# Routed experts in blocks of 32 slots on four column strips of the matrix array instead of blocks of 64 on two

## The reference, cut to what matters

```python
logits = xf @ w_router + b_router
top_val, top_idx = lax.top_k(logits, TOP_K)            # 4 of 32
top_w = jax.nn.softmax(top_val, axis=-1)
...
def expert_block(args):                                # the tokens of one expert, padded
    xb, e = args
    gate = xb @ w_gate[e] + b_gate[e]
    up = xb @ w_up[e] + b_up[e]
    gate = jnp.minimum(gate, SWIGLU_LIMIT)
    up = jnp.clip(up, -SWIGLU_LIMIT, SWIGLU_LIMIT)
    glu = gate * jax.nn.sigmoid(SWIGLU_ALPHA * gate)
    return ((up + 1.0) * glu) @ w_down[e] + b_down[e]
...
y = jnp.zeros((N, D)).at[tok_sorted].add(rows * w_sorted[:, None])
```

## Time and profile before

| | |
|---|---|
| median of 3 runs | 2026.03 us (2024.24 to 2029.33) |
| the profiled execution, its own time | 2019.1 us |
| its span in the trace | 2017.4 us |
| mean granted clock of TensorE, share of 2.4 GHz | 0.929 |
| experts' stage, first gate matmul to VectorE's last sum | 879.7 to 1985.0 us |
| TensorE busy / weight loads busy / VectorE / ScalarE | 89% / 47% / 32% / 15% |
| read from HBM | 486.86 MB |

### The profile page before, as it was taken

The page is one execution under the profiler, slowest core; times in us unless marked ns, Lnnn a source line. Parts: engine busy times, 40 slices in busy tenths (PEclk is TensorE's granted clock), DMA queues, the critical chain, the costliest instruction groups (busy, mean ns, idle before and its releaser), DMA issues. The chain is left out here.

```text
span 2017.4 us, 22708 instructions
## 1 busy us (share of the span) xinstructions
PE 1803.5 (89%) x8638; PEld 940.3 (47%) x8639; DVE 637.8 (32%) x1142; ACT 301.3 (15%) x521; POOL 126.1 (6%) x198
## 2 busy tenths in 40 slices
PE   6997998999879994589999999999999999999996
PEld 4775766868446762553333333333333333333332
DVE  1454333361410024733133333322332212232222
ACT  2234131110111001121011111111110100111002
POOL 1111202112100005200000000000000000000000
PEclk8998999997689997699998999999999999999997
DMA  9352162210255332049899999998999779898720
GB/s 325 129 167 84 42 233 101 84 53 1 61 184 206 117 147 96 0 192 421 311 379 414 421 422 422 422 422 342 417 417 390 298 292 365 311 410 336 250 83 28
DMA packets 114943, 494.07 MB, mean 245 GB/s; under 512 B 9931, under 2 KB 27532, under 8 KB 65687
## 3 DMA queue, kind: packets, MB, share of 16 engines
q1 hardware_dynamic: 112906, 490.69, 62.8%
q10 hardware_dynamic: 1984, 2.64, 0.4%
HBM read 486.86 MB, written 6.43 MB: 245 GB/s over the span
## 5 line engine op out<-in xcount | busy, mean ns | idle before, releaser
L1710 PE MATMUL ps_moe<-ring,hT_moe 128*64 128x512 f32 x1280 | 308.6, 641 | 0.0
L1710 PE MATMUL ps_moe<-ext,xg 128*64 128x512 f32 x1280 | 281.8, 595 | 3.5 <-DVE xg L1809 3.5
L1710 PE MATMUL ps_moe<-ring,xg 128*64 128x512 f32 x1280 | 281.7, 595 | 0.0
L739 PE MATMUL ps_mix<-hT,ring 128*128 128x320 f32 x896 | 263.2, 450 | 14.7 <-ACT cbuf L656 6.7
L739 PEld LDWEIGHTS ps_mix<-hT,ring 128*128 128x128 f32 x896 | 174.9, 198 | 90.7 <-issue 15.8
L1710 PEld LDWEIGHTS ps_moe<-ring,hT_moe 128*64 128x64 f32 x1280 | 95.4, 147 | 187.6 <-issue 185.0
L1710 PEld LDWEIGHTS ps_moe<-ext,xg 128*64 128x64 f32 x1280 | 91.8, 137 | 180.5 <-issue 177.5
L1710 PEld LDWEIGHTS ps_moe<-ring,xg 128*64 128x64 f32 x1280 | 89.2, 137 | 178.4 <-issue 178.3
L1836 DVE TENSOR_SCALAR gate<-ps_moe 128x1024 f32<-128x1024 f32 x32 | 39.2, 1224 | 233.7 <-PE ps_moe L1717 233.7
L1845 DVE TENSOR_SCALAR hid<-ps_moe 128x512 f32<-128x512 f32 x64 | 44.0, 687 | 209.8 <-PE ps_moe L1717 209.8
L1822 DVE TENSOR_SCALAR chosen<-ones,expert_row 96x64 bf16<-96x64 f32 x32 | 8.0, 250 | 313.8 <-PE ps_moe L1717 313.8
(11 more groups left out here) (354 smaller groups left out, 1711.1 us busy)
## 6 DMA issues: line engine op xcount, KB each, us to landing
ext<-in_w_gate SPq DMA_DIRECT2D x128, 1024.0 KB, 9.9
ring<-in_w_up SPq DMA_DIRECT2D x128, 1024.0 KB, 10.9
ring<-in_w_down SPq DMA_DIRECT2D x128, 1024.0 KB, 8.4
ring<-in_w_in SPq DMA_DIRECT2D x18, 2048.0 KB, 9.1
ring<-in_w_ada SPq DMA_DIRECT2D x12, 2048.0 KB, 9.3
ext<-in_state_gdn_rec SPq DMA_DIRECT2D x8, 512.0 KB, 8.4
out_rec_sample<-ext SPq DMA_DIRECT2D x8, 512.0 KB, 3.2
ring<-in_w_branch_b SPq DMA_DIRECT2D x2, 2048.0 KB, 15.0
```

What stands on the lines that cost most here:

```text
L739: last = nc.tensor.matmul(out, ring[:, place(i), k, P * j:P * j + P], rhs[:, k, :], start=k == 0, stop=k == NC - 1)
L1710: last = nc.tensor.matmul(ps[MID * a:MID * a + MID, bank + blk, :], lhs(blk, c), w[:, k, HALF * a:HALF * a + HALF], start=c == 0, stop=False)
```

## The change

The block of tokens becomes 32 slots wide (STRIP = 32, four blocks in CAP), and each matmul takes a quarter of the output columns (QW = 256) to one of four 32-column strips of the array. A block's product is then 8 chunks by 4 strips. Every PSUM tile of 128 by 512 holds two blocks of 128 by 256. The number of blocks is chosen among 1, 2 and 4: block 1 runs if there are more than 32 tokens, blocks 2 and 3 if there are more than 64, and block 0 always and last. Only block 0 signals that a piece is used. The scatter sums work on four row strips of 32 slots each; they always add blocks 0 and 1, and 2 and 3 for over 64 tokens. The hidden transposes and the put transposes are always made for all four blocks; the put transposes are split in two parts, of which the second stands behind the down product. `sig` shares its memory with `hid`, and `slots` lies in an older buffer.

```diff
-MID = CAP // 2
+NBLK = CAP // STRIP
+Q = NSTRIP
+QW = D // Q
...
-                            for blk in range(blocks):
-                                for a in range(2):
-                                    last = nc.tensor.matmul(ps[MID * a:MID * a + MID, bank + blk, :], lhs(blk, c),
-                                                            w[:, k, HALF * a:HALF * a + HALF], start=c == 0, stop=False)
...
-                        last.then_inc(piece_t, 1)
+                def strips(m, bank, blk, lhs, wait):
+                    for c in range(NC):
+                        if c % 2 == 0:
+                            wait(4 * m + c // 2)
+                        w = raw_piece(ring, ext, 4 * m + c // 2)
+                        for q in range(Q):
+                            last = nc.tensor.matmul(ps[STRIP * q:STRIP * q + STRIP, bank + blk // 2,
+                                                       QW * (blk % 2):QW * (blk % 2) + QW],
+                                                    lhs(blk, c), w[:, c % 2, QW * q:QW * q + QW], start=c == 0, stop=False)
+                        if blk == 0 and c in (1, 3, 5):
+                            last.then_inc(piece_t, 1)
...
+                def product(i, m, bank, n_tok, b, lhs, ready=None):
+                    with pe.If(n_tok > CAP * b + STRIP):
+                        block_of(i, m, bank, 1, lhs, ready)
+                    with pe.If(n_tok > CAP * b + 2 * STRIP):
+                        for blk in (2, 3):
+                            block_of(i, m, bank, blk, lhs, ready)
+                    block_of(i, m, bank, 0, lhs, ready).then_inc(piece_t, 1)
+
+                def sums(i, j, banks, n_tok, b):
+                    def block(blk):
+                        for q in range(Q):
+                            last = nc.tensor.matmul(ps[:, banks[q], 0:T], yrow[STRIP * q:STRIP * q + STRIP, blk, P * j:P * j + P],
+                                                    put[STRIP * q:STRIP * q + STRIP, blk, :], start=blk == 0, stop=blk == 1)
+                        return last
+                    block(0)
+                    with pe.If(n_tok > CAP * b + 2 * STRIP):
+                        block(2)
+                        block(3)
+                    block(1).then_inc(comb_t, 1)
...
                 def body(i, e, b, first_of_pass):
-                    by_width(mine, lambda blocks: product(i, 0, 0, blocks, ...
-                        by_width(before, lambda blocks: first_pairs(i - 1, blocks))
-                    by_width(mine, lambda blocks: product(i, 1, 2, blocks, ...
-                        by_width(before, lambda blocks: last_pairs(i - 1, blocks, True))
+                    product(i, 0, 0, mine, b, of_x)
+                        first_sums(i - 1, before, b)
+                    product(i, 1, 2, mine, b, of_x)
+                        last_sums(i - 1, before, b, True)
+                    turn_hidden(i)
+                        pe.wait_ge(comb_s, 3 * i)
+                    turn_put(0)
+                    product(i, 2, 4, mine, b, ...
+                    pe.wait_ge(put_s, 2 * i + 1)
+                    turn_put(1)
```

More of the change, by code:

```diff
@@ L1686, in body @@
[L1686 to L1693, removed]
+                    for n, (blk, bank) in enumerate(((0, 2), (1, 5), (2, 3))):
+                        act.wait_ge(turn_t, 3 * i + n + 1)
+                        k = 2 if blk == 2 else 1
+                        nc.scalar.activation(hT[:, blk:blk + k], ps[:, bank, 0:2 * P * k].rearrange(
+                            "p (b j s) -> p b j s", b=k, j=2), ACT.Copy).then_inc(hT_s, 1)
@@ L1695, in _, with epilogue @@
+                    take_put(i, 0)
+                def epilogue(b):
+                    take_rows(b * E + E - 1)
+                    take_put(b * E + E - 1, 1)
+                over_passes(act, body, lambda b: None, epilogue)
             @block.tensor
             def _(pe):
-                def product(i, m, bank, blocks, lhs, ready=None):
-                    for q in range(4):
-                        p = 4 * m + q
-                        pe.wait_ge(raw_full[p], 16 * (i + 1))
[L1703 to L1707, removed]
-                            for blk in range(blocks):
-                                for a in range(2):
-                                    last = nc.tensor.matmul(ps[MID * a:MID * a + MID, bank + blk, :], lhs(blk, c),
-                                                            w[:, k, HALF * a:HALF * a + HALF], start=c == 0, stop=False)
[L1712 to L1718, removed]
-                        last.then_inc(piece_t, 1)
@@ new lines, in block_of, with wait @@
+                def block_of(i, m, bank, blk, lhs, ready):
+                    def wait(p):
+                        pe.wait_ge(raw_full[p], 16 * (i + 1))
+                        if ready and p == 4 * m:
+                            ready(blk)
+                    strips(m, bank, blk, lhs, wait)
+                    if m == 0:
+                        pe.wait_ge(chosen_s, i + 1)
+                    for q in range(Q):
+                        last = nc.tensor.matmul(ps[STRIP * q:STRIP * q + STRIP, bank + blk // 2, QW * (blk % 2):QW * (blk % 2) + QW],
+                                                chosen[0:3 * E, :], brow[0:3 * E, m, QW * q:QW * q + QW], start=False, stop=True)
+                    return last
@@ L1742, in turn_hidden @@
[L1742 to L1751, removed]
@@ L1756, in turn_put, with tokens @@
+                def turn_put(part):
+                    for blk in (2 * part, 2 * part + 1):
                         for tau, (t0, n) in enumerate(TILE):
-                            last = nc.tensor.transpose(ps[:, 6 + blk, t0:t0 + n], wpick[0:n, tau, blk, :], ident[0:n, 0:n])
+                            last = nc.tensor.transpose(ps[:, 6 + blk % 2, t0:t0 + n], wpick[0:n, tau, blk, :], ident[0:n, 0:n])
                     last.then_inc(put_t, 1)
[L1760 to L1764, removed]
+                def tokens(e):
+                    return pe.value_load(count[0:1, bass.ds(e, 1)], min_val=0, max_val=T)
@@ L1766, in body @@
                 def body(i, e, b, first_of_pass):
-                    wide = lambda e: pe.value_load(count[0:1, bass.ds(e, 1)], min_val=0, max_val=T) > CAP * b + MID
-                    mine = wide(e)
+                    mine = tokens(e)
                     pe.wait_ge(xg_s, i + b + 1)
-                    by_width(mine, lambda blocks: product(i, 0, 0, blocks, lambda blk, c: xg[:, c, MID * blk:MID * blk + MID]))
+                    of_x = lambda blk, c: xg[:, c, STRIP * blk:STRIP * blk + STRIP]
@@ L1826, in body @@
                     dve.wait_ge(cur_s, i + 1)
+                    if not start:
+                        dve.wait_ge(put_t, 2 * i)
                     if start:
```

108 lines of the change are left out of this document (56 added, 52 removed).

## The result

The changed kernel takes **2507.07 us** (median of 4 runs, 2499.01 to 2519.28) against 2025.13 us before: a ratio of 1.241 (95% interval 1.231 to 1.251), 482 us slower. The prediction was 1999 us with a range up to 2105. Its rival 1, the loop's code that no longer stays on the core, had 0.38 of the chance, and with 56 us above the median about a ninth of the price that it turned out to have.

The account below looks back on a forecast made before the run. TensorE alone was taken to bound the experts' stage, with loads nearly full. TensorE 922, load waits 133 and last sums 7.4 gave 1063; plus 15 for clock against 1105, 27 us less: 1999 us, own range 1987 to 2018, 8 in 10 1987 to 2105.

Parts of the forecast that it names:

- rival 1: Experts' loop: code touching eight packets no longer stays on the core; stage 46 us longer, 2082 us; chance 0.38.
- The products: Each expert's gate, up and down products: 0.216 us a round of four, 3.65 us for up to 32 tokens.
- rival 2: Products: short matmuls limited by issue, 0.25 us a round, 4.1 us a block; about 2030 us; chance 0.17.
- Sums and transposes: Between and behind an expert's products: sums 1.28 us, up to down 5.52, put transposes 1.2.
- TensorE's own time: Per expert: 18.9 us up to 32 tokens, 29.6 for 33 to 64, 51.1 above; 922 in all.
- The count of the body: Experts' loop body: grows from 792 to 1840 instructions, seven packets and more, touching eight.
- The loads and the clock: Experts' stage: waits for weights of 98 and 35 us, stage 1063 us, plus 15 us for low clock.
- the forecast's term for code: Experts' loop: the forecast's sum, 1063 + 15 - 1105, 27 us less, had no time for fetching code.
- The jump at 3.6 us: Jumps to code not held: 3.6 us each, from two skipped passes at the stage's end costing 7.2 us.
- The cover: Jumps in small experts: queued work hides part of the stop at the up product, leaving 1.7 us.
- The clock at 10 us: Experts' stage with code fetched again: 10 us allowed for low clock, within the 2082 us.
- What would show it: Signs in the profile: if code is refetched, hundreds of queue 8 packets in the loop and unexplained idle before gate products.

Follow-up runs that it names:

- the kernel with one block of 64: Changed kernel with tokens 65 to 128 of an expert in one block of 64 on two strips, not two of 32 on four: 2004.49 us, ratio 0.990.
- aligned kernel with cut loads: Changed kernel, block 2 tested separately, one 64 block above 96 tokens, body starting at a 16 KB border, weight loads cut to an eighth: 1809.89 us.
- changed kernel with cut loads: Changed kernel with each weight piece's load cut to the first 128 of 1024 columns: 2233.09 us.
- the best kernel here: Changed kernel, block 2 tested separately, one 64 block above 96 tokens, body starting at a 16 KB border, all work done: 1938.92 us, ratio 0.960.

## Why the prediction was wrong, point by point

*What bounds the kernel now*: right, and confirmed wherever the code was held (29.8 us for a small expert in a row of small ones, with waits for weights).

*The products*: right. 3.57 us was the sum, 3.57 was measured in wide experts, and 3.70 with the step to the next operation (1366.98 to 1370.68) where 3.65 was taken. A round of four takes 0.216 us, so there is a matmul every 54 ns on average. Of rival 2 nothing is left: the floor of about 62 ns without hardware decode that the Trainium skill gives in "TensorE: Matmul & The Clock Gate" (Wait — 56ns, not 53.3ns?) does not bind here, and its 25 ns cannot be seen.

*Sums and transposes*: right within 0.4 us. Sums 1.29 (1.28 taken), from up to down 5.93 (5.52), put transposes behind down 1.14 (1.2).

*TensorE's own time*: 18.9, 29.6 and 51.1 were taken; 20.6, 30.8 and about 51.5 measured (the last in experts 23 and 25 of the kernel with one block of 64). Most of the 1.7 us of a small one is a down product of 4.75 us, in part at 1.2 GHz, behind the thin transposes. The sum is 957 instead of 922.

*The count of the body*: 1840, by four instructions for every float32 operation, is 40 too high for its 20 transposes, which leave one matmul record and one weight load each, and lacks the waits and branches. The trace has 1832, and the conclusion of eight touched pieces stands.

*The loads and the clock*: right in kind. The kernel with one block of 64 has the forecast's work for every size but 0.6 us of put transposes. Its stage, first gate matmul to last sums, is 882.7 to 1971.0 = 1088 us, where the forecast had 1063 + 15 = 1078, and 2004 us in all against 1999 predicted. That the two are so near is in part luck: TensorE's own time was 35 us too low, and this hardly shows, because a small expert in a row of small ones takes the 29.8 us of its loads either way.

**The step that failed is the forecast's term for code, which was nothing.** The sum 1063 + 15 - 1105 takes it that the loop's code stays on the core. It did not: the stops measured 470 us in the stage, and the low clock behind them about 140 more. The reason given for putting them into rival 1, at 0.38, was "against it, that no row shows a limit". There was no row for the limit, but there was the Trainium skill's "Runtime: NRT & Kernel Launch" (instruction fetch mechanics), which gives TensorE 128 KiB, filled in blocks of 16 KiB. Read as eight pieces, one of them for the piece fetched ahead, that agrees with the runs: seven touched pieces are held, eight are not. The same section also says that a taken branch to a target outside a window of two pages has to wait for a fetch; this the runs do not bear out for TensorE, since the kernel before jumps back over some three pieces and fetched nothing in thirty rounds. So the page did not settle the matter alone. But the prediction's own count had the body touch eight pieces, it said itself that by that reading the time would be this rival's, and no row spoke against it: that should have had most of the chance.

**And the price of rival 1 was mis-sized.** It gave 221 us of stops, 10 for the clock and a stage 46 us longer. The stage became 1578 us (887.0 to 2465.4), 473 longer:

| term | rival 1 as predicted | measured |
|---|---|---|
| TensorE's own work | 922 | 957 (19 x 20.6 + 5 x 30.8 + 8 x 51.5) |
| stops for code | 221 (9.5, 4.5, 2.3 us an expert) | 470 (medians 20.3, 10.6, 4.6) |
| low clock | 10 | about 140, an estimate (busy time above that of the aligned kernel with cut loads, 5.7 and 4.0 us an expert, and some 2 above the changed kernel with cut loads for a wide one) |
| last sums | 7 | 7 |
| sum | 1160 | 1574 (the stage: 1578) |

- *The jump at 3.6 us* came from the end of the stage, where the loads were over. With an eighth of the loads the small expert's stops measure 11.0 against 9.5 taken; under the full loads they are 20.3. The row was of the right event at the wrong time: in the loop the weights come at 250 GB/s on average beside the fetches.
- *The cover* was too optimistic. I let queued work hide part of the up product's stop (5.0 measured, 1.7 taken) and counted none in the down product (3.8).
- *The clock at 10 us* was the habit of the forecast, in which idle time lies behind loads and a low clock costs nothing. With stops that are on TensorE's own path, each comes with a stretch at 1.2 GHz after it, also on the path: 0.82 over the stage against 0.97.

*What would show it* worked: hundreds of packets in queue 8 in the loop, idle time ahead of gate products that no load explains. But "wide experts take over 53 us" would have been the quicker sign (56 to 60, with the stop ahead of them).

*What nobody had asked*: whether the new block size is used where it pays. Three blocks in place of four for the experts of 65 to 96 tokens is 10.5 us for each of seven of them, and the largest part of what the best kernel here gains.

## What to carry to other kernels

Before a hardware loop grows, count TensorE's instructions in it (four for a float32 matmul here) and the 16 KB pieces that the body touches at the address where it will lie. With eight the loop fetched its code again nearly every round, with seven it did not, and 112 instructions ahead of the loop made a difference of 448 us; a rarely taken branch counts in full. Price a stop from a stretch in which the same other traffic runs, and add the low clock that follows it.

## What the runs showed of the hardware

- TensorE kept loop bodies of up to 1666 instructions in seven pieces of 16 KB, without a packet from 975 us until the stage's end, and fetched again, mostly nine packets a round, with eight touched. This agrees with the 128 KiB that the Trainium skill's "Runtime: NRT & Kernel Launch" (instruction fetch mechanics) states for TensorE, if one of its eight blocks is the one fetched ahead; no run isolates that.
- A stop at the loop's jump back is 4.6 us under full loads and 2.8 us with an eighth of them (medians over the wide experts).
- A test and a jump over held code cost next to nothing: with 96 more of them the kernel took 2030.88 against 2023.16 us (one run each).
- Code executed straight on, outside what is held, cost nothing visible: blocks of 136 instructions followed each other every 3.57 us in wide experts while packets came.
